# Giving half of the down-weight remainder to GpSimd in a mixture-of-experts stage

## The reference

```python
hg = jnp.einsum('td,edf->tef', xt, w_gate)     # d = 1024, f = 256
hu = jnp.einsum('td,edf->tef', xt, w_up)
act = jax.nn.silu(hg) * hu * gates[..., None]
return jnp.einsum('tef,efd->td', act, w_down)  # back to d = 1024
```

## Time and profile before

| what | value |
|---|---|
| median of three runs | 1527.59 us (1525.78 to 1533.89) |
| profiled execution, its own time | 1527.91 us |
| span of its trace | 1526.1 us |
| mean granted TensorE clock | 0.940 |
| busy, PE / PEld / DVE / ACT / POOL | 87% / 68% / 77% / 53% / 41% of the span |
| tiles of the experts | 48, from about 985 to 1462 us of the span |

### The profile page before, as it was taken

The page is one execution under the profiler, slowest core; times in us unless marked ns, Lnnn a source line. Parts: engine busy times, 40 slices in busy tenths (PEclk is TensorE's granted clock), DMA queues, the critical chain, the costliest instruction groups (busy, mean ns, idle before and its releaser), DMA issues. The chain is left out here.

```text
span 1526.1 us, 24485 instructions
## 1 busy us (share of the span) xinstructions
PE 1325.4 (87%) x7142; PEld 1034.2 (68%) x7142; DVE 1170.3 (77%) x2127; ACT 810.7 (53%) x1662; POOL 622.8 (41%) x720
## 2 busy tenths in 40 slices
PE   5999999989997889799999994399999999999910
PEld 2688888856665556577777773278887888888700
DVE  3888888846775777466666664989999999999838
ACT  2432333213336568244444442278888888888733
POOL 1117666732226830012122111246666666566400
PEclk9999999979999999899999997599999999999955
DMA  9423444389977542344433446936798887985697
GB/s 332 130 99 133 173 175 158 147 298 356 311 232 196 168 152 86 131 138 138 137 137 137 160 146 202 313 87 164 204 266 257 236 245 200 270 222 108 155 332 284
DMA packets 138446, 298.24 MB, mean 195 GB/s; under 512 B 22244, under 2 KB 79717, under 8 KB 135886
## 3 DMA queue, kind: packets, MB, share of 16 engines
q1 hardware_dynamic: 110550, 218.63, 41.7%
q0 software_dynamic: 20800, 61.13, 17.2%
q10 hardware_dynamic: 7024, 17.60, 3.2%
HBM read 305.18 MB, written 102.25 MB: 267 GB/s over the span
## 5 line engine op out<-in xcount | busy, mean ns | idle before, releaser
L2753 DVE TENSOR_TENSOR ex_w_lo<-route_wgu,ex_w_hi 128x1024 fp32r<-128x1024 f32 x192 | 225.9, 1219 | 3.8 <-ACT ex_w_hi L2577 3.1
L2577 ACT ACTIVATE ex_w_hi<-route_wgu 128x1024 fp32r (+1 forms) x192 | 193.1, 1066 | 3.3 <-issue 3.2
L146 PE MATMUL ex_ps_h<-ex_w_hi,ex_xT 128*128 128x512 f32 x384 | 156.9, 409 | 6.1 <-DVE ex_x_lo L2782 5.9
L2540 POOL DMA_INDIRECT scratch_acc<-route_o,ex_to x48 | 91.8, 1912 | 156.0 <-DMA scratch_acc<-route_o,ex_to 79.0
L148 PE MATMUL ex_ps_h<-ex_w_hi,ex_x_lo 128*128 128x512 f32 x384 | 151.4, 394 | 0.0
L147 PE MATMUL ex_ps_h<-ex_w_lo,ex_xT 128*128 128x512 f32 x384 | 150.7, 393 | 0.0
L146 PE MATMUL fr_ps_m<-fr_whi,fr_hl 128*128 128x512 f32 (+1 forms) x384 | 138.7, 361 | 0.9 <-DVE fr_wlo L657 0.5
L148 PE MATMUL fr_ps_m<-fr_whi,fr_hl 128*128 128x512 f32 (+1 forms) x384 | 136.1, 354 | 0.0
L147 PE MATMUL fr_ps_m<-fr_wlo,fr_hl 128*128 128x512 f32 (+1 forms) x384 | 135.9, 354 | 0.0
L2027 POOL TENSOR_SCALAR mx_st<-mx_st 128x1 f32<-128x1 f32 x68 | 29.3, 432 | 256.9 <-ACT mx_j L2071 148.7
L2790 DVE TENSOR_TENSOR ex_wd_lo<-route_wd,ex_wd_hi 128x1024 fp32r<-128x1024 f32 x96 | 113.8, 1227 | 8.3 <-ACT ex_wd_hi L2595 6.4
(11 more groups left out here) (489 smaller groups left out, 3468.8 us busy)
## 6 DMA issues: line engine op xcount, KB each, us to landing
route_wgu<-in_w_exp_gate_dram SPq DMA_DIRECT2D x48, 1024.0 KB, 14.4
route_wgu<-in_w_exp_up_dram SPq DMA_DIRECT2D x48, 1024.0 KB, 17.7
route_wd<-in_w_exp_down_dram SPq DMA_DIRECT2D x48, 1024.0 KB, 9.7
scratch_rec<-fr_w SPq DMA_DIRECT2D x16, 1112.0 KB, 4.2
s_rec<-scratch_rec SPq DMA_DIRECT2D x32, 556.0 KB, 6.2
scratch_proj<-fr_io SPq DMA_DIRECT2D x16, 640.0 KB, 3.0
scratch_acc<-in_zeros_dram SPq DMA_DIRECT2D x18, 512.0 KB, 5.8
fr_w<-in_w_ada_dram SPq DMA_DIRECT2D x8, 1024.0 KB
```

The costliest lines, as they stand in the source:

```text
L146: nc.tensor.matmul(out, hi, w_hi, start=first, stop=False)
L2540: pool.indirect_dma_start(T["acc"], bass.IndirectOffsetOnAxis(to[:, t:t + 1], 0), o[:, t % 2, :], None, compute_op=ALU.add).then_inc(sem(" ...
L2577: A(w_hi[:, par, c * PW:(c + 1) * PW], wgu[:, bass.ds(slot * (KD * 2 * DE) + c * PW, PW)], ACT.Copy).then_inc(S["w_rounded"], 1)
L2753: vec.tensor_tensor(w_lo[:, par, c * PW:(c + 1) * PW], wgu[:, bass.ds(slot * (KD * 2 * DE) + c * PW, PW)], w_hi[:, par, c * PW:(c + 1) * P ...
```

## The change

For each tile, GpSimd makes the remainder of the first block of the down weights (`wd_lo[:, 0, :]`), and VectorE only that of the second. GpSimd does it before the scatter-add of the tile before. VectorE's wait, which was one per block, becomes a single wait for both rounded blocks. TensorE's `down` waits for both engines.

```diff
+            def split_d(t):
+                slot = pool.value_load(plan[0:1, 2, t:t + 1], min_val=0, max_val=NSL - 1)
+                pool.wait_ge(S["d_rounded"], t * 2 + 1)
+                nc.gpsimd.tensor_tensor(wd_lo[:, 0, :], wd[:, bass.ds(slot * (2 * D), D)], wd_hi[:, 0, :].bitcast(F32), ALU.subtract).then_inc(S["d_split_g"], 1)
+
             pool.wait_ge(S["to_ready"], 1)
+            pool.wait_ge(S["planned"], 1)
+            split_d(0)
             for t in range(NTILE):
                 if t + 2 < NTILE:
                     weigh(t + 2)
                 if t + 2 < NTILE - U:
                     refill(t + 2)
+                if t + 1 < NTILE:
+                    split_d(t + 1)
                 store(t)
...
             def split_d(t, slot):
                 dve.wait_ge(S["a_moved"], t + 1)
                 vec.scalar_tensor_tensor(a_lo[:, :, :], ps_a[:, 0:2 * P].rearrange("p (k n) -> p k n", k=2), 0.5, a_hi[:, :, :].bitcast(F32), ALU.mult, ALU.subtract).then_inc(S["a_split"], 1)
-                for k in range(2):
-                    dve.wait_ge(S["d_rounded"], t * 2 + k + 1)
-                    vec.tensor_tensor(wd_lo[:, k, :], wd[:, bass.ds(slot * (2 * D) + k * D, D)], wd_hi[:, k, :].bitcast(F32), ALU.subtract).then_inc(S["d_split"], 1)
+                dve.wait_ge(S["d_rounded"], t * 2 + 2)
+                vec.tensor_tensor(wd_lo[:, 1, :], wd[:, bass.ds(slot * (2 * D) + D, D)], wd_hi[:, 1, :].bitcast(F32), ALU.subtract).then_inc(S["d_split"], 1)
...
             def down(t):
                 pe.wait_ge(S["a_moved"], t + 1)
                 pe.wait_ge(S["a_split"], t + 1)
-                pe.wait_ge(S["d_split"], t * 2 + 2)
+                pe.wait_ge(S["d_split"], t + 1)
+                pe.wait_ge(S["d_split_g"], t + 1)
```

More of the change, by code:

```diff
@@ L2405, in moe @@
         junk = wd[:, 3 * D:4 * D]
-        names = ("x2_in G2_in G2_samples eps_set tailed tail_out weighed wt_ready to_ready summed rooted rstd g_ready y_ready y_out cleared5 consts5 w5_in mm5 mod5 row5 out5 ident_in step de exped hot counted planned matched turned rows_ready x_flipped x_moved_a x_moved_v w_rounded w_split d_rounded d_split a_split gu_done th_ready "
+        names = ("x2_in G2_in G2_samples eps_set tailed tail_out weighed wt_ready to_ready summed rooted rstd g_ready y_ready y_out cleared5 consts5 w5_in mm5 mod5 row5 out5 ident_in step de exped hot counted planned matched turned rows_ready x_flipped x_moved_a x_moved_v w_rounded w_split d_rounded d_split d_split_g a_split gu_done th_ready "
                  "sg_ready a_ready a_flipped a_moved d_done o_out_a st_even st_odd").split()
```

## The result

The changed kernel takes 1577.84 us (1574.53 to 1583.57, four runs) against 1530.74 us for the kernel before (1525.78 to 1537.26, four runs): ratio 1.0309, 95% interval 1.0252 to 1.0366, some 47 us slower. The forecast was slower, but 1553.5 us with a range of 1535 to 1575. The sign and the first mechanism held; the change in time was nearly twice the one forecast.

What follows compares the result with a forecast made beforehand. TensorE and VectorE were taken as nearly full in the expert stage. 22 us for the periods, 0.7 at the start and 3.3 at the end gave +26 on 1527.9, hence 1554, stated as 1553.5 us; range 1535 to 1575.

Steps and rivals of the forecast that it cites:

- the first mechanism: GpSimd's SBUF subtraction blocks VectorE's instructions with two SBUF inputs, so one `wd_lo` or its follower takes 2 to 3.3 us.
- VectorE's queue of 9.19 us: VectorE's instructions for one tile without gaps, from `x_lo` to gate, in the kernel before: 9.19 us.
- The hold: Time per tile that GpSimd's subtraction keeps VectorE from two-SBUF-input work: 2.1 us, bounds 2.0 and 2.35.
- the queue at 9.82: Period if VectorE's `w_lo` pair sets the subtraction's start: 2.27 + 2.1 + 5.45 = 9.82 us.
- whether GpSimd can keep up: GpSimd's loop per tile put at 9.6 us, under the 10.0 period; the store, some 3 us later, hidden.
- The 45 periods: Distances between the 46 tiles of the expert stage, 10.0 us each instead of 9.51: 22 us more, bounds 13 to 36.
- The period: Time per tile in the expert stage: 10.0 us, bounds 9.8 to 10.3, partly for tiles where GpSimd comes late.
- The end: Last stores wait only for each other; one stands behind a GpSimd subtraction, the next subtraction is hidden: +3.3 us.
- The single wait: VectorE's wait for both rounded blocks: nothing with the hold; without it up to 0.8 us, hidden behind TensorE.
- Rival 1: GpSimd's subtraction hides beside gate and `x_lo`, TensorE is the bound: period 9.34 to 9.39, 1523 to 1526 us, chance 0.06.
- Rival 3: The hold partly replaces waits VectorE had anyway: period 9.6 to 9.7 us, time 1536 us, chance 0.12.
- Rival 2: GpSimd becomes the bound, waiting a full VectorE instruction per subtraction: period 10.7 us, time 1585 us, chance 0.12.

Runs made afterwards that it cites:

- double_sub: The loads_early kernel with GpSimd's subtraction made twice per tile, the second after the first is done: 1660.6 us, ratio 1.0837.
- loads_early: The changed kernel with VectorE's and ScalarE's register loads of slot numbers moved to the start of each step: 1557.8 us, ratio 1.0172.
- mid_store: The kernel before, with the scatter-add of tile t waiting for the first of VectorE's two down subtractions of tile t+1: 1537.6 us, ratio 1.0030.
- small_sub: The changed kernel with GpSimd subtracting only 8 of the 1024 columns, the rest of that remainder left out: 1537.9 us, ratio 1.0049.
- late_store: The kernel before, with the scatter-add of tile t waiting for both of VectorE's down subtractions of tile t+1: 1539.3 us, ratio 1.0044.

## Why the prediction was wrong

**Where it was right.** The bound of the kernel before; VectorE's queue of 9.19 us and the 1.13 taken from it; that GpSimd's subtraction shuts VectorE out, at the place given (after the first half of `w_lo`, with `a_lo` beside it); GpSimd not the bound; TensorE at 93% (94 given). The hold was put at 2.1 and is 2.2 by the timeline and by double_sub; the queue at 9.82, measured 9.95.

**The step that failed** is in the paragraph on whether GpSimd can keep up: of the scatter-add it says that it "goes out some 3 us later" and "this is hidden". It was priced only by its buffer. What it does when it moves was not asked: VectorE's register loads issued in the 2 to 5.5 us behind it take up to 1.4 us, and it was moved so that this stretch covers VectorE's load ahead of `w_lo`. Long loads cost 0.44 us per tile, 20 of the 47 us, as loads_early shows by taking them away (VectorE's and ScalarE's together); mid_store shows that moving the scatter-add brings the gap without the subtraction. The 45 periods were put at 22 us more and took 41. The trace of before had the long loads (26 of 86 on VectorE), but a register load does not count as busy time in the profile, and the prediction has no term for it.

**The period** was put at 10.0, and with the loads out of the way it is 10.02. That agreement is partly luck. The 0.2 above the forecast's 9.82 stood for tiles in which GpSimd comes late. In loads_early it is something else: VectorE waits for ScalarE's second block in 42 of 43 tiles, 22 us in all, and part of the hold passes meanwhile, so `wd_lo` has 2.58 us in the median instead of 3.10.

**The end** was mis-sized: 3.3 us forecast, 6.3 measured. The forecast delayed one scatter-add; all were late by then, so the chain of landings began one link earlier.

**The single wait** was put at nothing with the hold there and as hidden without it. The first holds in most tiles (4 waits, 4.8 us). The second does not: the forecast had up to 0.8 us, hidden behind TensorE, and in small_sub VectorE waits for it in 42 tiles, 48 us in all (1.15 each), with a period of 9.70. How much of that period is this wait and how much long loads of ScalarE is open.

**The rivals.** Rival 1 is refuted by `wd_lo` at 3.10 us. Rival 3 had the hold vanish into VectorE's waits, with a period of 9.6 to 9.7; with the long loads out of the way it is 10.02. (Its 1536 is the low end of its own terms, which give 1536 to 1540.) Rival 2's time, 1585, is nearer to the measured 1577.84 than the forecast's, but by chance: GpSimd waits for ScalarE in 28 tiles, and loads_early takes 20 us away with GpSimd's work unchanged.

## What to carry to other kernels

An elementwise piece given to GpSimd is not taken from VectorE if GpSimd reads SBUF while VectorE has instructions with two SBUF operands to run: here 1.13 us went and a hold of 2.2 came, of which 0.33 passed beside `a_lo`. When a DMA issued by GpSimd moves in time, ask what else happens at that distance behind it, on every engine, register loads included. A load of a register whose value is known a step ahead is best issued where the queue behind it is full and no scatter-add has just gone out; the same move gains in one order and costs in another, so it is to be placed by the trace.

## What the runs showed of the hardware

Between 1030 and 1430 us, register loads (TENSOR_LOAD) of all engines mostly take 0.27 to 0.32 us, but up to 1.4 us on VectorE and 1.6 on SyncE in the changed kernel (1.7 on ScalarE in small_sub) if issued 2 to 5.5 us after the start of the scatter-add with accumulation that GpSimd issues; outside this stretch at most three are long in any of the kernels. Not every load in the stretch is long. Where it begins differs: of the loads issued 2.0 to 2.5 us after the scatter-add's start 27 of 35 are long in small_sub, where its issue takes 1.6 us, and 3 of 16 in late_store, where it takes 2.3.

What the loads wait for is not shown. The scatter-add's own packets are a candidate: in the changed kernel they begin to move about 3 us after its start, in small_sub about 2.5. At the starts of VectorE's long loads in the changed kernel 15.7 packets of the queue with GpSimd's DMAs are in flight on average, at those of the short ones 5.1 (before: 13.2 and 7.0). But these packets go on until some 8 us after the start, well beyond the stretch. No run tells cause from mere timing here.
